# A two-block transformer kernel: one more weight unit split ahead of the wait for x, and TensorE's first feed-forward loop pass written out

## The chip, the cores and the metric

The kernel runs on one NeuronCore of one Trainium2 chip. The metric is the device time of one execution in microseconds; three executions gave 1204.47 to 1204.54, median 1204.53. One further execution was recorded by the hardware profiler and took 1204.95.

## The reference, cut to what matters

Two transformer stages run one after the other on 256 tokens of width 1024, all in fp32. The change touches only the four feed-forward layers, of which the first opens the kernel.

```python
def swiglu(x, w_gate, w_up, w_down):
    return (jax.nn.silu(x @ w_gate) * (x @ w_up)) @ w_down

# first block, D_FF = 2816, FFN_RES = 0.5
h = h + FFN_RES * swiglu(rms_norm(h, ffn1_norm[l]), ffn1_w_gate[l], ffn1_w_up[l], ffn1_w_down[l])
h = h + hybrid_mixer(...)
h = h + FFN_RES * swiglu(rms_norm(h, ffn2_norm[l]), ...)
# second block, two layers, each: mixer, cross-attention, then
x = x + swiglu_2(rms_norm_2(x, g_ffn[layer]), w_gate[layer], w_up[layer], w_down[layer])
```

## The kernel before, in words

Weights come in **units**: 128 partitions by 1024 fp32 values (512 KB), numbered from 0 in the order in which TensorE uses them (TOTAL of them, table STREAM). Each unit passes four hands. SyncE (SP) loads it into a raw slot, in a feed-forward one of six (`loaded[slot]` rises by 32 when both halves are in). ScalarE (ACT) rounds it to the high part `wh` (L741, `high_done`). VectorE (DVE) subtracts to get the low part `wl` (L1360, `low_done`). TensorE then runs 12 matmuls of 512 columns on it (L2035 to L2037: high by high, high by low, low by high) and raises `units_used`. `wh` and `wl` have six slots (NSPLIT), so unit u may be split once unit u - 6 is used. In the code `split(v)` of ScalarE adds LEAD = 4 to v, so `split(u + 2)` with u = 0 is unit 6, the seventh; VectorE's order is the same.

A feed-forward layer has 11 chunks (NFC) of 256 hidden columns. A chunk takes 4 gate/up units and 2 down units. After the gate/up units of a chunk, ScalarE does the SiLU (`silu_step`, L845, two instructions, scaled by `rstd`), VectorE multiplies by the up half (`mul_step`, L1423, which writes `sb_scores` and raises `h_ready` twice a chunk), ScalarE makes two uint16 planes (`planes_step`), a DMA transposes them, VectorE joins them (L1434), ScalarE makes the high part `hTh` and VectorE the low part `hTl` (L1440, `ht_low`). TensorE then uses them on the down units.

TensorE's order in a layer is: gate/up of chunk 0, of chunk 1 (bank 0), then `body(0)` (gate/up of chunk 2 in bank 6, down of chunk 0), then a loop whose pass c does the gate/up of chunk c + 2 in bank 0 and the down units of chunk c. Each loop pass starts with a wait for `h_ready`, so that the bank it overwrites has been read. In the loop that wait is for the value 2·NFC·f + 4 + 2c, in pass 1 the value 6: chunk 2 multiplied. Bank 0, which pass 1 overwrites, holds chunk 1. `start` and `stop` of the accumulation groups, all slots and all other waits are set by constants or by the loop register.

In layer 0 (f = 0) the beginning is special. Units 0 to 5 come from a packed tensor `h_first`, then SP loads x (two halves, `x_in` 16 each), then units 6 and 7 and on. ScalarE splits units 0 to 5, and then needs x for the sum of squares of each token (`token_ssq`, L784, two instructions). GpSimd (POOL) turns the sums into `rstd` (L619, L620), on which `silu_step(0)` waits. All queues are in order: SP's, ScalarE's, VectorE's and TensorE's instructions run in the order in which they stand.

Of the kernel before, what the change touches and what calls it, by code (L numbers as in the profile page):

```python
# [36 lines left out]
NFC = FF // FC  # L37
# [105 lines left out]
def two_block_kernel(nc, d, out):  # L143
    ctx = ExitStack()
    with ctx:
# [3 lines left out]
        def sem(name):  # L149
            return ctx.enter_context(nc.semaphore(name))  # L150
# [157 lines left out]
        h_ready = sem("h_ready")  # L308
# [422 lines left out]
        def _(act):  # L731
# [8 lines left out]
            def copy(dst, src, scale=1.0):  # L740
                return act.activation(dst, src, ACT.Copy, scale=scale)  # L741

            def split(u, c=0):

                u = u + LEAD
                if isinstance(c, int):
                    u, c = u + 6 * c, 0
                    if u >= TOTAL:
                        return

                act.wait_ge(loaded[SLOT[u]], 32 * NTH[u] + 32 * c)
                if u >= NSPLIT:

                    act.wait_ge(units_used, u - NSPLIT + 1 + 6 * c)
                copy(wh[:, u % NSPLIT, :], raws[SLOT[u]]).then_inc(high_done, 1)

            def splits(u, n):
                for i in range(n):
                    split(u + i)
# [27 lines left out]
            def rs(stat, t):  # L787
                return rstd[:, 2 * stat + t:2 * stat + t + 1]
# [51 lines left out]
            def ffn(f, tail=None):  # L840
                u, norm = FIRST[f"ffn{f}"], FFN_NORM[f]

                def silu_step(c, first_bank=0):
                    for t in range(NT):
                        act.activation(silu[:, t, :], bank[first_bank + t][:, 0:FC], ACT.Silu, scale=rs(norm, t))\  # L845
                           .then_inc(silu_done, 1)

                def planes_step(c):

                    act.wait_ge(h_ready, 2 * NFC * f + 2 + 2 * c)  # L850
                    for h in range(2):
                        ins = copy(planes.rearrange("p (h t c) -> p h t c", h=2, t=NT)[:, h], hid_halves[:, h])
                    ins.then_inc(planes_done, 1)

                def turned_step(c, dst):

                    act.wait_ge(hT_joined, NFC * f + c + 1)
                    copy(dst, hT).then_inc(ht_high, 1)

                def turn_hidden():  # L860
                    act.dma_start_transpose(planesT.rearrange("p (b r) -> p b r", r=P), planes).then_inc(planes_turned, 16)

                def hidden(c, v, c6=0):

                    split(v, c6)
                    planes_step(c)

                    act.wait_ge(planes_done, NFC * f + c + 1)
                    split(v + 1, c6)
                    turn_hidden()  # L870

                def body(c, last=False):
                    v = u + 8
                    split(v, c)
                    split(v + 1, c)
                    turned_step(c, hTh[:, :, :])
                    split(v + 2, c)
                    split(v + 3, c)
                    if last:
                        turned_step(c + 1, yTh[:, 6:8, :])  # L880

                    act.wait_ge(units_used, v + 4 + 6 * c)
                    silu_step(c + 2)
                    hidden(c + 2, v + 4, c)

                if f > 0:
                    xt_high(norm, 0)
                    if f > 1:

                        splits(u - 2, 2)  # L890
                    xt_high(norm, 1)
                split(u)
                if f > 0:
                    token_ssq(norm, x)
                    load_tables(SILU_SET)
                split(u + 1)
                if f == 0:

                    act.wait_ge(x_in, 32)
                    token_ssq(norm, x)  # L900
                    split(u + 2)
                rstd_known(norm)

                act.wait_ge(units_used, u + 4 if f > 0 else u + 5)
                silu_step(0, FFN_FIRST_BANK[f])
                n = 2 if f > 0 else 3
                hidden(0, u + n)
                if f == 2:
                    km_split(1, 4)
                    split(u + 4)  # L910
                    km_turn(1)
                for i in range(4 if f in (1, 3) else 5, 8):
                    split(u + i)

                act.wait_ge(units_used, u + 8)
                silu_step(1)
                turned_step(0, hTh[:, :, :])
                hidden(1, u + 8)
                splits(u + 10, 2)

                act.wait_ge(units_used, u + 12)
                silu_step(2, 6)
                hidden(2, u + 12)
                with act.Fori(1, NFC - 3, 1) as c:
                    body(c)
                body(NFC - 3, True)
                split(u + 62)
                turned_step(NFC - 1, aTh[:, 6:8, :])
                split(u + 63)
                if tail is not None:  # L930
                    tail()
                splits(u + 64, 2)
# [1096 lines left out]
        def _(pe):  # L2029
# [85 lines left out]
            def ffn(f, norm_after):  # L2115
                u, norm = FIRST[f"ffn{f}"], FFN_NORM[f]
                acc = [[bank[2 + 2 * n + t] for n in range(2)] for t in range(NT)]

                def down(u_slot, k, n, t, start, stop, high, low):
                    w = slice(512 * n, 512 * n + 512)  # L2120
                    return products(acc[t][n][:, :], high[:, k, tok(t)], low[:, k, tok(t)],
                                    wh[:, u_slot % NSPLIT, w], wl[:, u_slot % NSPLIT, w], start, stop)

                def gate_up(v, bank_, c=0, begun=0):

                    for i in range(begun, 4):
                        square(v + i, 2 * i, aTh, aTl, bank_, i == 0, i == 3, c)

                def down_unit(v, k, high, low, c=0, start=False):

                    pe.wait_ge(low_done, v + 1 + 6 * c)
                    for n in range(2):
                        for t in range(NT):
                            ins = down(v, k, n, t, start, False, high, low)
                    ins.then_inc(units_used, 1)

                def body(c, bank_=0, start=False):
                    if bank_ == 0:

                        pe.wait_ge(h_ready, 2 * NFC * f + 4 + 2 * c)  # L2140
                    gate_up(u + 8, bank_, c)

                    pe.wait_ge(ht_low, NFC * f + 1 + c)
                    for k in range(2):
                        down_unit(u + 12 + k, k, hTh, hTl, c, start and k == 0)

                if f == 0:
                    for i in range(EARLY):
                        early_unit(i, (FFN_FIRST_BANK[f], 0)[FRONT[i][0]], 2 * FRONT[i][1])
                    chunk(u + 1, FFN_FIRST_BANK[f], a_ready(norm), begun=2)  # L2150
                    gate_up(u + 4, 0, begun=1)

                    pe.wait_ge(ident_in, 16)
                else:
                    chunk(u, FFN_FIRST_BANK[f], a_ready(norm), before={1: lambda: xt_half(norm, 1)})
                    gate_up(u + 4, 0)
                body(0, 6, True)
                with pe.Fori(1, NFC - 3, 1) as c:
                    body(c)
                body(NFC - 3)  # L2160

                pe.wait_ge(ht_low, NFC * f + NFC - 1)
                for k in range(2):
                    down_unit(u + 62 + k, k, yTh[:, 6:8, :], yTl[:, 6:8, :])

                pe.wait_ge(ht_low, NFC * f + NFC)

                pe.wait_ge(low_done, u + 66)
                for n in range(2):
                    for t in range(NT):  # L2170
                        if n == 1 and t == 1 and norm_after is not None:
                            xt_half(norm_after, 0)
                        for k in range(2):
                            ins = down(u + 64 + k, k, n, t, False, k == 1, aTh[:, 6:8, :], aTl[:, 6:8, :])
                            if n == 1 and t == 1:
                                ins.then_inc(units_used, 1)
                        if n == 0 or t == 0:
                            ins.then_inc(acc_done, 1)
# [495 lines left out]
```

## Time and profile before

| | before |
|---|---|
| median of 3 executions | 1204.53 us |
| profiled execution | 1204.95 us |
| its span, first to last instruction | 1203.0 us |
| TensorE busy | 1195.1 us, 99% |
| VectorE busy | 780.0 us, 65% |
| ScalarE busy | 699.0 us, 58% |
| GpSimd busy | 73.8 us, 6% |
| DMA, mean | 195 GB/s |

The span is what the profiler's instructions cover; the profiled execution lasted 1.95 us longer. Busy time of TensorE contains the modelled end of each matmul (0.39 us shown for one, while the next starts 0.227 us after it), so where a start comes late, the step between two starts tells more than the idle time that the profile reports.

### The profile page before, as it was taken

How to read it: one execution, taken by the hardware profiler on the slowest of the kernel's cores; microseconds unless marked ns; L12 is line 12 of the kernel's file. 1: busy time of each engine (PE TensorE's matmuls, PEld its weight loads, DVE VectorE, ACT ScalarE, POOL GpSimd, SP SyncE). 2: the span in 40 equal slices, each digit the busy share in tenths (PEclk: the TensorE clock that was granted, in tenths of full speed). 3: DMA queues.
4: the chain of work that ended last, by engine and by line, in shares of the span. 5: the costliest groups of instructions: out<-in, count | busy, mean ns of one | idle time of the engine just before them, and what ended most of it. 6: DMA issues, size and time to landing. Idle time of an engine off the chain costs nothing.

```text
span 1203.0 us, 16864 instructions
## 1 busy us (share of the span) xinstructions
PE 1195.1 (99%) x5622; PEld 986.0 (82%) x5622; DVE 780.0 (65%) x1107; ACT 699.0 (58%) x1030; POOL 73.8 (6%) x119
## 2 busy tenths in 40 slices
PE   9999999999999999999999999999999999999998
PEld 7888888877788888888888788888888887888887
DVE  6656556688686656557778766756556667665554
ACT  7545555566555545558675576645555546755552
POOL 0430000000000000000220110000000000000000
PEclk9999999999999999999999999999999999999999
DMA  9987764554556987755754528977655454876662
GB/s 314 268 235 228 224 200 153 162 168 139 164 193 190 275 248 231 220 179 174 200 171 162 175 60 230 262 226 210 205 175 175 144 163 132 245 225 200 202 200 76
DMA packets 218917, 234.68 MB, mean 195 GB/s; under 512 B 66608, under 2 KB 158896, under 8 KB 218864
## 3 DMA queue, kind: packets, MB, share of 16 engines
q1 hardware_dynamic: 163792, 214.61, 56.9%
q10 hardware_dynamic: 53280, 13.64, 6.3%
q0 software_dynamic: 1792, 5.75, 1.7%
q8 instruction: 31, 0.51, 0.2%
q14 instruction: 22, 0.18, 0.0%
HBM read 219.78 MB, written 1.05 MB: 184 GB/s over the span
## 4 chain that ended last, share of the span: by engine, by line
PE 96%; DMA 2%; DVE 1%; ACT 1%; issue 0%; ACTq 0%; DVEq 0%
PE bank L2035 30%; PE bank L2037 30%; PE bank L2036 30%; PE bank L2094 2%; DMA sb_probs<-sb_probs 1%; PE bank L2248 1%; PE bank L2264 1%; PE bank L2235 1%; PE bank L2233 0%; DMA sb_gates<-h_xT 0%; ACT sb_probs L1277 0%; PE bank L2552 0%; DVE sb_rmax L1930 0%; PE bank L2541 0%; PE bank L2266 0%
## 5 line engine op out<-in xcount | busy, mean ns | idle before, releaser
L1360 DVE TENSOR_TENSOR sb_wl<-sb_raw,sb_wh 128x1024 fp32r<-128x1024 f32 x313 | 376.3, 1222 | 116.5 <-ACT sb_wh L741 111.6
L2035 PE MATMUL bank<-sb_wh,sb_aTh 128*128 128x512 f32 (+1 forms) x1124 | 435.5, 387 | 0.6 <-DVE sb_scores L1423 0.5
L2037 PE MATMUL bank<-sb_wh,sb_aTl 128*128 128x512 f32 (+1 forms) x1124 | 431.0, 383 | 0.0
L2036 PE MATMUL bank<-sb_wl,sb_aTh 128*128 128x512 f32 (+1 forms) x1124 | 430.7, 383 | 0.0
L741 ACT ACTIVATE sb_wh<-sb_raw 128x1024 fp32r<-128x1024 f32 (+1 forms) x319 | 326.9, 1047 | 142.2 <-PE bank L2037 103.0
L2035 PEld LDWEIGHTS bank<-sb_wh,sb_aTh 128*128 128x128 f32 x1124 | 211.3, 188 | 42.2 <-issue 1.4
L2037 PEld LDWEIGHTS bank<-sb_wh,sb_aTl 128*128 128x128 f32 x1124 | 211.2, 188 | 41.9
L2036 PEld LDWEIGHTS bank<-sb_wl,sb_aTh 128*128 128x128 f32 x1124 | 211.4, 188 | 40.1
L1360 DVE TENSOR_TENSOR sb_wl<-sb_z,sb_wh 128x1024 fp32r<-128x1024 f32 x88 | 107.5, 1226 | 56.0 <-ACT sb_wh L741 56.0
L845 ACT ACTIVATE sb_junk<-bank,sb_rstd 128x256 f32<-128x256 f32 x88 | 36.8, 470 | 156.6 <-PE bank L2037 156.3
L1423 DVE SCALAR_TENSOR_TENSOR sb_scores<-bank,sb_rstd,sb_junk 128x256 f32<-128x256 f32 x88 | 38.5, 479 | 115.6 <-ACT sb_junk L845 115.4
L2035 PE MATMUL bank<-sb_wh,sb_hTh 128*128 128x512 f32 x288 | 112.0, 389 | 0.0
L2036 PE MATMUL bank<-sb_wl,sb_hTh 128*128 128x512 f32 x288 | 112.0, 389 | 0.0
L2037 PE MATMUL bank<-sb_wh,sb_hTl 128*128 128x512 f32 x288 | 112.0, 389 | 0.0
L741 ACT ACTIVATE sb_wh<-sb_z 128x1024 fp32r<-128x1024 f32 x88 | 92.8, 1059 | 1.7 <-DMA sb_z<-h_first 0.5
L2035 PE MATMUL bank<-sb_wh,sb_yTh 128*128 128x512 f32 x224 | 89.8, 401 | 0.0
L2037 PE MATMUL bank<-sb_wh,sb_yTl 128*128 128x512 f32 x224 | 87.5, 390 | 0.0
L2036 PE MATMUL bank<-sb_wl,sb_yTh 128*128 128x512 f32 x224 | 87.3, 390 | 0.0
L2036 PEld LDWEIGHTS bank<-sb_wl,sb_hTh 128*128 128x128 f32 x288 | 54.1, 188 | 11.3
L2035 PEld LDWEIGHTS bank<-sb_wh,sb_hTh 128*128 128x128 f32 x288 | 54.0, 188 | 11.2
L2037 PEld LDWEIGHTS bank<-sb_wh,sb_hTl 128*128 128x128 f32 x288 | 54.1, 188 | 11.2
L741 ACT ACTIVATE sb_probs<-sb_scores 128x512 uint16<-128x512 uint16 x88 | 50.4, 625 | 3.3 <-DVE sb_scores L1423 3.2
(220 smaller groups left out, 929.1 us busy)
## 6 DMA issues: line engine op xcount, KB each, us to landing
sb_raw<-ffn_w_down SPq DMA_DIRECT2D x80, 256.0 KB, 4.4
sb_raw<-w_in SPq DMA_DIRECT2D x80, 256.0 KB, 3.2
sb_raw<-w_down SPq DMA_DIRECT2D x80, 256.0 KB, 3.9
sb_raw<-w_gate SPq DMA_DIRECT2D x48, 256.0 KB, 3.2
sb_raw<-w_up SPq DMA_DIRECT2D x48, 256.0 KB, 4.0
sb_raw<-ffn_w_gate SPq DMA_DIRECT2D x44, 256.0 KB, 3.6
sb_raw<-ffn_w_up SPq DMA_DIRECT2D x44, 256.0 KB, 4.4
sb_raw<-e_w_in SPq DMA_DIRECT2D x40, 256.0 KB, 3.3
```

Of the source, the lines that this page charges most:

```text
L741: return act.activation(dst, src, ACT.Copy, scale=scale)
L845: act.activation(silu[:, t, :], bank[first_bank + t][:, 0:FC], ACT.Silu, scale=rs(norm, t))\
L1360: dve.tensor_tensor(wl[:, u % NSPLIT, :], raws[SLOT[u]], wh[:, u % NSPLIT, :].bitcast(F32), ALU.subtract).then_inc(low_done, 1)
L1423: dve.scalar_tensor_tensor(hid[:, t, :], bank[first_bank + t][:, FC:2 * FC], rs(norm, t), silu[:, t, :], ALU.mult, ALU.mult).then_inc(h_re ...
L2035: pe.matmul(dst, lh, w_hi, start=start, stop=False)
L2036: pe.matmul(dst, lh, w_lo, start=False, stop=False)
L2037: return pe.matmul(dst, ll, w_hi, start=False, stop=stop)
L2094: ins = pe.transpose(dst[:, T * j + P * t:T * j + P * t + P], tiles(j, t), ident[:])
L2235: pe.matmul(bank[4 + i % 2][:, P:3 * P], q[:, P:T], k[:, 0:T], start=True, stop=True).then_inc(at.s_psum, 1)
L2248: ins = pe.transpose(bank[6][:, tok(j)], probs[:, i % 4, tok(j)], ident[:])
L2264: pe.matmul(bank[7][r, a:a + T], v[:, 0, c], pT[:, 0:T], start=True, stop=False)
```

## The change

On ScalarE, in layer 0, the split of unit 6 now stands before the wait for x and the two sums of squares instead of behind them. On TensorE, in all four layers, pass 1 of the loop is written out as straight code, and its wait is for `h_ready` at 2·NFC·f + 4 (chunk 1 multiplied), a constant; the loop runs from pass 2.

```diff
                 split(u + 1)
                 if f == 0:
+                    split(u + 2)
 
                     act.wait_ge(x_in, 32)
                     token_ssq(norm, x)
-                    split(u + 2)
                 rstd_known(norm)
...
                 def body(c, bank_=0, start=False):
-                    if bank_ == 0:
+                    if isinstance(c, int) and c == 1:
+
+                        pe.wait_ge(h_ready, 2 * NFC * f + 4)
+                    elif bank_ == 0:
 
                         pe.wait_ge(h_ready, 2 * NFC * f + 4 + 2 * c)
                     gate_up(u + 8, bank_, c)
...
                 body(0, 6, True)
-                with pe.Fori(1, NFC - 3, 1) as c:
+                body(1)
+                with pe.Fori(2, NFC - 3, 1) as c:
                     body(c)
                 body(NFC - 3)
```

ScalarE at the front of layer 0, as a difference of the two orders (the first two rows are units 4 and 5, the L741 row that moves is unit 6, L784 the sums of squares, L845 the SiLU of chunk 0):

```order
 L741 ACTIVATE sb_wh<-sb_z 128x1024 [waits loaded4]
 L741 ACTIVATE sb_wh<-sb_z 128x1024 [waits loaded5]
+L741 ACTIVATE sb_wh<-sb_raw 128x1024 [waits units_used,loaded0]
 L784 ACTIVATE sb_junk,sb_ssq<-sb_x 128x1024 [waits x_in]
 L784 ACTIVATE sb_junk,sb_ssq<-sb_x 128x1024 [waits ssq_done]
-L741 ACTIVATE sb_wh<-sb_raw 128x1024 [waits units_used,loaded0]
 L845 ACTIVATE sb_junk<-bank,sb_rstd 128x256 [waits units_used,rstd_ready]
 L845 ACTIVATE sb_junk<-bank,sb_rstd 128x256
```

Only this one instruction moved, with its waits for the load of unit 6 and for a used slot. The orders of VectorE and SP are the same in both kernels.

TensorE in layer 0 where `body(0)` ends and pass 1 begins, before:

```order
 L2035 MATMUL bank5<-sb_wh,sb_hTh 128x512
 L2036 MATMUL bank5<-sb_wl,sb_hTh 128x512
 L2037 MATMUL bank5<-sb_wh,sb_hTl 128x512
 L2158 UNCONDITIONAL_BRANCH
 L2158 ISA
 L2042 ISA [waits h_ready]
 L2035 MATMUL bank0<-sb_wh,sb_aTh 128x512 [waits low_done]
```

The same place after:

```order
 L2035 MATMUL bank5<-sb_wh,sb_hTh 128x512
 L2036 MATMUL bank5<-sb_wl,sb_hTh 128x512
 L2037 MATMUL bank5<-sb_wh,sb_hTl 128x512
 L2035 MATMUL bank0<-sb_wh,sb_aTh 128x512 [waits low_done,h_ready]
 L2036 MATMUL bank0<-sb_wl,sb_aTh 128x512
 L2037 MATMUL bank0<-sb_wh,sb_aTl 128x512
```

The loop's entry now stands one pass (72 matmuls) later; the matmuls executed are the same in number and order.

## Rows read from the trace of the kernel before

**Rows 1.** The page: the span, busy times, the granted TensorE clock in 40 slices.
```profile
span 1203.0 us, 16864 instructions
PE 1195.1 (99%) x5622; PEld 986.0 (82%) x5622; DVE 780.0 (65%) x1107; ACT 699.0 (58%) x1030; POOL 73.8 (6%) x119
PEclk9999999999999999999999999999999999999999
```

**Rows 2.** Waits of TensorE, whole span: waited for: us in total, times, longest.
```profile
PE bank L2541 <- DVE sb_probs L1944: 2.1, 4, 0.8
PE bank L2035 <- DVE sb_scores L1423: 0.5, 1, 0.5
```

**Rows 3.** Timeline of TensorE, layer 0: start us, us, instruction [idle before].
```profile
1.31 3.78 PE L2192 MATMUL bank<-sb_hTh 128*128 128x512 f32 x8 [1.31 <-POOL sb_half_neg L609]
...
22.30 0.39 PE L2037 MATMUL bank<-sb_wh,sb_aTl 128*128 128x512 f32 x1
22.77 0.50 PE L2035 MATMUL bank<-sb_wh,sb_aTh 128*128 128x512 f32 x1
23.11 0.40 PE L2036 MATMUL bank<-sb_wl,sb_aTh 128*128 128x512 f32 x1
...
28.39 0.39 PE L2035 MATMUL bank<-sb_wh,sb_aTh 128*128 128x512 f32 x1
...
39.27 0.39 PE L2035 MATMUL bank<-sb_wh,sb_hTh 128*128 128x512 f32 x1
...
44.48 0.39 PE L2037 MATMUL bank<-sb_wh,sb_hTl 128*128 128x512 f32 x1
45.34 0.49 PE L2035 MATMUL bank<-sb_wh,sb_aTh 128*128 128x512 f32 x1 [0.47 <-DVE sb_scores L1423]
```

**Rows 4.** Timeline of VectorE, layer 0: units 6, 7, 8, then 34 to 38 us.
```profile
21.49 1.23 DVE L1360 TENSOR_TENSOR sb_wl<-sb_raw,sb_wh 128x1024 fp32r<-128x1024 f32 x1 [3.98 <-ACT sb_wh L741]
...
23.51 1.23 DVE L1360 TENSOR_TENSOR sb_wl<-sb_raw,sb_wh 128x1024 fp32r<-128x1024 f32 x1
25.82 1.23 DVE L1360 TENSOR_TENSOR sb_wl<-sb_raw,sb_wh 128x1024 fp32r<-128x1024 f32 x1 [1.08 <-ACT sb_wh L741]
...
34.20 0.81 DVE L1434 COPY sb_probsT<-sb_probs 128x512 uint16<-128x512 uint16 x2 [3.46 <-DMA sb_probs<-sb_probs]
34.88 0.87 DVE L1423 SCALAR_TENSOR_TENSOR sb_scores<-bank,sb_rstd,sb_junk 128x256 f32<-128x256 f32 x2
...
36.65 1.23 DVE L1360 TENSOR_TENSOR sb_wl<-sb_raw,sb_wh 128x1024 fp32r<-128x1024 f32 x1 [0.25 <-ACT sb_wh L741]
```

**Rows 5.** Busy time in 1060 to 1190 us: length, PE, PEld, DVE, ACT, POOL, PEclk, DMA, GB/s.
```profile
1060.00:1190.00 130.00, 130.00 (x575) 107.67 (x574) 75.18 (x90) 66.40 (x86) 0.00 (x0) 1.00 0.63 190
```

**Rows 6.** TensorE's loop line: duration ns min/median/max, first and last start.
```profile
L2158 PEldq COMPARE_BRANCH  x28: 76/208/236, 57.9 to 1168.4; - x28
```

**Rows 7.** Timeline of ScalarE, layer 0, 18 to 25 us.
```profile
18.17 1.06 ACT L784 ACTIVATE sb_junk<-sb_x 128x1024 f32<-128x1024 f32 x1 [1.92 <-DMA sb_x<-x]
...
20.41 1.04 ACT L741 ACTIVATE sb_wh<-sb_raw 128x1024 fp32r<-128x1024 f32 x1
21.69 0.84 ACT L845 ACTIVATE sb_junk<-bank,sb_rstd 128x256 f32<-128x256 f32 x2 [0.23 <-POOL sb_rstd L620]
22.42 1.06 ACT L741 ACTIVATE sb_wh<-sb_raw 128x1024 fp32r<-128x1024 f32 x1
23.54 1.15 ACT L741 ACTIVATE sb_probs<-sb_scores 128x512 uint16<-128x512 uint16 x2
24.72 1.06 ACT L741 ACTIVATE sb_wh<-sb_raw 128x1024 fp32r<-128x1024 f32 x1
```

**Rows 8.** Timeline of SP's queue: the issue of unit 6's second half.
```profile
11.43 0.47 SPq L488 DMA_DIRECT2D sb_raw<-ffn_w_up  x1
```

**Rows 9.** DMA issues from 11.42 to 11.90 us: KB each, us to landing.
```profile
sb_raw<-ffn_w_up SPq DMA_DIRECT2D x1, 256.0 KB, 8.2
```

**Rows 10.** The chain that ended last, from 24 us: the first transpose.
```profile
24.73 9.44 DMA sb_probs<-sb_probs
```

## The prediction

> **What bounds the kernel now.** I read the page first: TensorE is busy 1195.1 of 1203.0 us, at the full clock in every slice [rows 1]. So a change pays only where it removes a late start of a matmul, and costs only where it makes one. Next I read who TensorE waits for. In the feed-forward layers there is a single entry, 0.5 us on VectorE's multiply; the larger ones are in the cross-attention [rows 2], which the change doesn't touch. Then the timeline of layer 0, by the steps between starts. Undisturbed, 48 matmuls run from 28.39 to 39.27, which is 0.2267 each and 2.72 per unit of 12. Two steps are longer. At unit 6 the step is 22.77 - 22.30 = 0.47, late by 0.24, and the matmul behind it comes after 0.34 instead of 0.227, another 0.11. At pass 1 the step is 45.34 - 44.48 = 0.86, late by 0.63 [rows 3]; I add 0.11 for the restart there too, after unit 6's. Together 0.35 + 0.74 = 1.09 us is all that the two edits can give back.
>
> **The wait at pass 1 (second edit).** In layer 0 pass 1 waits for chunk 2 multiplied; it now waits for chunk 1, multiplied at 34.88 + 0.87 = 35.75 [rows 4], over 9 us before TensorE gets there. The other wait there, for unit 14, was no bar: no further idle time follows it. So the edit takes 0.74 off as long as chunk 1 is in time. In layers 1 to 3 no such step exists, and from 1060 to 1190 us, nearly the whole loop of layer 3 and what follows it, TensorE is busy 130.00 of 130.00 [rows 5]. There is nothing to take there: 0.
>
> **The pass written out.** It removes one taken branch and a few register instructions per layer, 4 in all, and adds no executed matmul. Branches take 0.21 us median, 0.24 at most [rows 6], yet there are seven per layer (28 in all), and the stretch of layer 3 shows no idle time [rows 5]: they are decoded while matmuls already queued run. I take 0. From below the bound is 4 x 0.24 = 0.96 us gained, if each had been exposed; from above I take the same 0.96 us as a loss, one such stall per layer for fetching the longer code. The value is 0, for the straight code of `body(0)` runs at 0.2267 per matmul as the loop does [rows 3, 5]. The Trainium skill (Runtime: NRT & Kernel Launch, Instruction fetch mechanics) says that a taken branch to a target outside the fetched window stalls the engine, which is why kernels prefer unrolling. By that rule four stalls go and the sum below would come out near zero instead; the trace disagrees, with 130.00 busy of 130.00 in looped code [rows 5].
>
> **The split of unit 6 ahead of x (first edit).** This step decides the sign. ScalarE is in order. Before, it waits for x until 18.17, does both sums of squares, and starts unit 6 at 20.41 [rows 7]. For the split to be free in front of x, unit 6 would have to be in by about 17. But SP issues it behind x: its second half goes out at 11.43 and lands 8.2 us later [rows 8, 9], at 19.6 to 19.7. Nothing that decides this landing is changed. So ScalarE now sits until 19.66, splits until about 20.65 (a following instruction starts about 0.98 after one of 1.06), and only then starts the sums of squares, which wait for nothing any more. They start 20.65 - 18.17 = 2.48 us late. The split itself ends 0.73 earlier.
>
> What follows, each row moved by 2.48:
> - The sums end 20.41 -> 22.89 and the SiLU of chunk 0 goes from 21.69 to 24.17. Before, the split of unit 6 ran in the 1.28 us in which GpSimd made `rstd`; that cover is now empty time.
> - Unit 7's split stands behind the SiLU: 22.42 -> 24.90 [rows 7]. Its low part starts 23.51 -> 25.99 and ends at 27.22 [rows 4].
> - Unit 6 itself: high part at about 20.65, low part at 21.95, wanted at 22.53. The late start of 0.35 is gone.
> - TensorE wants unit 7 at 22.53 + 2.72 = 25.25 and gets it at 27.22 + 0.05 = 27.27 (unit 6 began 0.05 behind its low part: 21.49 + 1.23 = 22.72, 22.77). Stall 2.02, restart 0.11: +2.13.
> - Unit 8 begins at 27.27 + 2.72 + 0.11 = 30.10, before 28.39. Its low part was ready at 25.82 + 1.23 = 27.05, now 29.53: 0.57 in hand.
> - Chunk 0's transpose. It took 9.44 from 24.73 [rows 10]; issued at 27.21 with the same 9.44 it lands at 36.65 instead of 34.17, and chunk 1 is multiplied by 38.2. `hTl` of chunk 0 and unit 12 (36.65 + 1.23 = 37.88 before [rows 4], 40.36 then) are wanted at 40.98, the 39.27 of before plus 1.71. 0.6 us in hand, and none of these has a price.
>
> At pass 1: 30.10 + 48 x 0.2267 + 24 x 0.2267 = 46.42. Before, pass 1 started at 45.34 and had 0.11 of restart. Here the second edit acts: chunk 1 is ready at 38.2, so there is no wait, while chunk 2 (a transpose later) would have come at about 45.2 + 2.5 = 47.7 and cost 1.3 with the old wait.
>
> **The sum.** First edit: -0.35 + 2.13 = +1.78. Second: -0.74. Writing out: 0. Net +1.04, or by starts 46.42 - 45.34 - 0.11 = +0.97; the two differ by rounding, and I take +1.0. Later waits are relative to TensorE and move along with it. The profiled execution took 1204.95, so its like would be 1205.95. The median runs are 0.42 shorter: 1204.53 + 1.0 = **1205.5 us**. A change of under 0.2%, 2.4 us, can't be told from none for this kernel; this is such a one, with a sign of slower.
>
> **Rivals.**
> *Both edits give what they can.* If unit 6 were in when ScalarE asks, or if the delayed sums were absorbed, the time would be 1204.53 - 1.09 = 1203.4. For it: unit 6's own wait does vanish, and the second edit is sound by itself. Against: an 8.2 us landing behind x, and only 25.67 - 24.74 = 0.93 us of lead of unit 7 over TensorE against 2.48 of delay [rows 3, 4, 9]. Chance 0.14.
>
> *Branches were exposed.* Then 0.96 us comes off the +1.0 and the time is 1204.57. For it only that a branch takes 0.2 us; against it the stretch without idle time. The skill's rule on branches, cited above, is this case. Chance 0.04.
>
> *More of the chain is late.* The 0.57 and 0.6 us in hand at units 8 and 12 are used up, for instance by a first transpose that takes 1 us longer still, as it would then run beside the loads of units 13 to 15. That adds 0.4 to 1.2: 1205.9 to 1206.7, say 1206.3. For it: the transpose did take 9.44 us under load. Against: it now starts when the load backlog of the front is over, so it should be shorter. Chance 0.12.
>
> *Slower beyond doubt: the clock falls.* A stall of 2.0 us at 25 us, where the longest of before within the kernel is 0.8 [rows 2] and the clock stayed at its high level of 2.4 GHz [rows 1]. If the granted clock falls to 1.2 GHz there, matmuls start 0.43 apart, as the first eight did (3.78 us for 8 with the last one's end [rows 3]), instead of 0.227. It took some 4 us of such matmuls to rise again after the start, so 9 or 10 matmuls lose 0.2 each: +1.9, and with +1.0 the sum is +2.9, or 1207.4. It decides once an idle stretch longer than any of before is enough to lower the clock. Against: all 40 slices at full clock despite waits, and 2 us is little more than twice what was borne. Chance 0.06. The Trainium skill (TensorE: Matmul & The Clock Gate, HAM oscillation — how this bites in real kernels) says that waits for data between bursts of matmuls let the clock drop to half; the trace has no idle stretch of 2 us, so it bears out neither side.
>
> **How the numbers follow.** My forecast 0.64, full gain 0.14, late chain 0.12, clock 0.06, exposed branches 0.04. The range runs from the full gain, 1203.4, to the upper part of the late chain, 1206.6; outside it lie the clock case and what is left of extra stalls. The unknown cost of the written-out pass, 0.96 either way, keeps the forecast within 1204.5 to 1206.5, inside the range. Faster by over 0.2% would need more than the two late starts hold: 0.01. Slower by over 0.2% is the clock case and the far tail of the late chain: 0.06. Within 0.2%: 0.93.
>
> **What would show it.** In the new timeline: ScalarE idle on the load of unit 6 until about 19.7; the sums of squares at about 20.7; the SiLU at 24.2; TensorE stopping at 25.25 for about 2.0 us on VectorE's low part of unit 7 (start 27.3); no late start at unit 6 and none at pass 1, which begins near 46.4; full clock throughout; from there on every landmark 1.0 later than before. Sums of squares still at 18.2 would make me wrong and the kernel 1.1 us faster; a start of pass 1 later than 47 would show the late chain; starts 0.43 apart behind 27 us the clock.

## The result and the profile after

The changed kernel took 1206.49 us, median of 22 runs (1205.10 to 1208.11), against 1204.49 for the kernel before in 22 runs (1203.49 to 1205.14): +2.0 us, ratio 1.0016 with a 95% interval of 1.0010 to 1.0022, or +1.2 to +2.7 us. The prediction was 1205.5 in a range of 1203.4 to 1206.6. The sign and the stall are as forecast, the size is twice it.

The page of the changed kernel, with the span and busy times (answers to [rows 1]):

```profile
span 1204.9 us, 16832 instructions
PE 1194.8 (99%) x5622; PEld 985.8 (82%) x5622; DVE 779.7 (65%) x1107; ACT 698.8 (58%) x1030; POOL 72.9 (6%) x119
```

TensorE does the same work in 1.9 us more of span. The waits of TensorE (us in total, times, longest; to [rows 2]) name two things in layer 0 that were not there:

```profile
PE bank L2545 <- DVE sb_probs L1944: 2.1, 4, 0.8
PE bank L2063 <- ACT sb_wh L741: 1.5, 1, 1.5
...
PE bank L2035 <- DVE sb_wl L1360: 1.3, 1, 1.3
```

The 1.3 us on `sb_wl` is the forecast stall. The 1.5 us on L2063 lies in the first 9 us, before anything that the change touches. The kernel before has that wait too, shorter in its profile, in a row that the prediction passed over when it read TensorE's waits:

```profile
PE bank L2063 <- ACT sb_wh L741: 0.6, 1, 0.6
```

The timelines of ScalarE and TensorE after (start us, us, instruction; to [rows 7] and [rows 3]):

```profile
20.34 1.06 ACT L741 ACTIVATE sb_wh<-sb_raw 128x1024 fp32r<-128x1024 f32 x1 [3.43 <-DMA sb_raw<-ffn_w_up]
21.31 1.04 ACT L784 ACTIVATE sb_junk<-sb_x 128x1024 f32<-128x1024 f32 x1
...
24.81 0.84 ACT L845 ACTIVATE sb_junk<-bank,sb_rstd 128x256 f32<-128x256 f32 x2 [1.19 <-POOL sb_rstd L620]
25.54 1.06 ACT L741 ACTIVATE sb_wh<-sb_raw 128x1024 fp32r<-128x1024 f32 x1
```

```profile
15.56 0.39 PE L2035 MATMUL bank<-sb_wh,sb_aTh 128*128 128x512 f32 x1
...
26.21 0.39 PE L2037 MATMUL bank<-sb_wh,sb_aTl 128*128 128x512 f32 x1
27.91 0.50 PE L2035 MATMUL bank<-sb_wh,sb_aTh 128*128 128x512 f32 x1 [1.31 <-DVE sb_wl L1360]
28.25 0.39 PE L2036 MATMUL bank<-sb_wl,sb_aTh 128*128 128x512 f32 x1
...
47.10 0.39 PE L2035 MATMUL bank<-sb_wh,sb_aTh 128*128 128x512 f32 x1
```

ScalarE sits 3.43 us on the load of unit 6, the sums of squares follow, and where GpSimd makes `rstd` ScalarE is now idle for 1.19 us instead of 0.23. TensorE stops ahead of unit 7 for 27.91 - 26.21 - 0.23 = 1.47 us, plus 0.11 at the restart. There is no late start at unit 6 nor at pass 1 (47.10). But unit 3 starts at 15.56, not 14.27: the whole front of this execution is 1.3 us later. This is not the change's doing: the second profile of the changed kernel, at the end, has unit 3 at 14.32. So the front varies from one execution to the next, which made me doubt the profile of before as the basis.

### The profile page after: what moved, and what is told of

Read it like the earlier page. It is cut to its first block, busy times and chain, and to the rows that moved or that the text cites. A ratio compares the mean times of both kernels' runs of the same rounds, so it can differ in the third digit from the quotient of the medians.

```text
span 1204.9 us, 16832 instructions
## 1 busy us (share of the span) xinstructions
PE 1194.8 (99%) x5622; PEld 985.8 (82%) x5622; DVE 779.7 (65%) x1107; ACT 698.8 (58%) x1030; POOL 72.9 (6%) x119
## 3 DMA queue, kind: packets, MB, share of 16 engines
q0 software_dynamic: 1792, 5.75, 1.6%
## 4 chain that ended last, share of the span: by engine, by line
PE 96%; SPq 1%; ACT 1%; DVE 1%; DMA 1%; issue 0%; POOL 0%; POOLq 0%
PE bank L2035 30%; PE bank L2037 30%; PE bank L2036 30%; PE bank L2094 2%; PE bank L2252 1%; DMA sb_raw<-ffn_w_up 1%; PE bank L2268 1%; PE bank L2239 1%; SPq L546 1%; PE bank L2237 0%; ACT sb_probs L1277 0%; PE bank L2556 0%; DVE sb_rmax L1930 0%; PE bank L2545 0%; PE bank L2270 0%
## 5 line engine op out<-in xcount | busy, mean ns | idle before, releaser
L741 ACT ACTIVATE sb_wh<-sb_raw 128x1024 fp32r<-128x1024 f32 (+1 forms) x319 | 326.6, 1047 | 145.7 <-PE bank L2037 105.5
L845 ACT ACTIVATE sb_junk<-bank,sb_rstd 128x256 f32<-128x256 f32 x88 | 37.0, 471 | 158.3 <-PE bank L2037 157.1
L741 ACT ACTIVATE sb_wh<-sb_z 128x1024 fp32r<-128x1024 f32 x88 | 92.8, 1059 | 1.7 <-DMA sb_z<-h_first 0.5
L741 ACT ACTIVATE sb_probs<-sb_scores 128x512 uint16<-128x512 uint16 x88 | 50.4, 626 | 2.1 <-DVE sb_scores L1423 2.1
```

## The experiments

"u3" below is the start of unit 3 on TensorE, the first matmul behind the three early units; "u6" is the landing of unit 6. From u3 to pass 1 there are 132 matmuls, 29.92 us undisturbed. Each time is a median of 11 runs (9 for the last), beside runs of the kernel before on the same chip. An interval of the ratio of 0.0009 either way is 1.1 us either way, so a difference of a few tenths can be read only from the traces.

One sum helps to read all of them. In 12 of the 14 profiles the profiled time less the start of pass 1 lies between 1159.4 and 1159.7 us, from 1204.95 - 45.34 for the first profile to 1206.82 - 47.10 for the changed kernel. So whatever these kernels gain or lose, they gain or lose before pass 1 of layer 0. The two exceptions are the two kernels under "An early front".

**Each edit alone.** First edit alone: only ScalarE's part of the diff.

```diff
                 if f == 0:
+                    split(u + 2)
 
                     act.wait_ge(x_in, 32)
                     token_ssq(norm, x)
-                    split(u + 2)
```

> First edit alone: unit 6 split ahead of the wait for x, loop and its wait as before. Theory (the delayed sums of squares stall TensorE on unit 7): unit 6's high part starts when its load lands, about 20 us, TensorE stops before unit 7 by 1.5 to 2.0 us and reaches pass 1 so late that chunk 2 is multiplied by then, so the old wait costs little; time as with both edits, 1206.0 to 1206.5 against 1204.5. Rival (the written-out pass carries part of the loss): 0.5 to 1.0 us less than with both edits, 1205.5 or below.

Measured: 1206.09 against 1204.52, ratio 1.0012 (1.0003 to 1.0021). The first edit alone carries the loss of about 1.6 us. Its trace has the same stop:

```profile
27.15 0.50 PE L2035 MATMUL bank<-sb_wh,sb_aTh 128*128 128x512 f32 x1 [1.26 <-DVE sb_wl L1360]
```

It starts 1.42 us late, and pass 1, with the old wait for chunk 2, starts without a gap at 46.34. The old wait costs nothing here: in this trace chunk 2 is multiplied by 44.23, over 2 us before TensorE arrives. The prediction had put it at 47.7, and 1.3 us of wait with it; but the two transposes, issued later, took 6.0 and 6.1 us to land and not 9.4 and 5.9.

Second edit alone: only TensorE's part of the diff.

```diff
-                    if bank_ == 0:
+                    if isinstance(c, int) and c == 1:
+                        pe.wait_ge(h_ready, 2 * NFC * f + 4)
+                    elif bank_ == 0:
...
-                with pe.Fori(1, NFC - 3, 1) as c:
+                body(1)
+                with pe.Fori(2, NFC - 3, 1) as c:
```

> Second edit alone: pass 1 written out with the wait for chunk 1, the split of unit 6 where it was. Theory: the late start at pass 1 (0.74 us with its restart) is gone, nothing else moves: 1203.8 against 1204.5. Rival (written-out code costs about 1 us somewhere): 1204.8 or more.

Measured: 1204.68 against 1204.52, ratio 1.0000 (0.9991 to 1.0009). My 0.7 us of gain did not show, though the interval of 1.1 us either way would still hold it. The trace says why there was nothing to gain in this execution: chunk 2 was multiplied by 43.29 and pass 1 began at 45.55, so the old wait would have been over as well. The time is near the rival's 1204.8, but the next kernel shows that its reason is not the one.

**Written out, old wait.**

```diff
-                with pe.Fori(1, NFC - 3, 1) as c:
+                body(1)
+                with pe.Fori(2, NFC - 3, 1) as c:
```

> Pass 1 written out, but with the old wait for chunk 2; split of unit 6 where it was. Theory: writing out is free, and the late start at pass 1 of about 0.6 us stays: 1204.5, no change. Rival (written-out code costs): 1205.0 to 1205.5.

Measured: 1204.58 against 1204.52, ratio 0.9999 (0.9990 to 1.0008). Straight code costs nothing that can be measured, nor do its four branches fewer bring anything. But its trace refutes the other half of my expectation: with the old wait there is no late start either. VectorE multiplies chunk 2 here (second row below) by 43.57, and pass 1 starts at 45.06, 29.92 behind u3 at 15.14:

```profile
42.02 0.81 DVE L1434 COPY sb_probsT<-sb_probs 128x512 uint16<-128x512 uint16 x2 [0.67 <-DMA sb_probs<-sb_probs]
42.70 0.87 DVE L1423 SCALAR_TENSOR_TENSOR sb_scores<-bank,sb_rstd,sb_junk 128x256 f32<-128x256 f32 x2
```

**Unit 6 loaded ahead of x.** Both edits, and on SP's queue:

```diff
+                load_gate_up(6, 0, FRONT[6][1], FRONT[6][0])
                 for t in range(NT):
                     sp.dma_start(x[:, t, :], xv[:, t, :]).then_inc(x_in, 16)
-                for u in range(6, 8):
-                    load_gate_up(u, 0, FRONT[u][1], FRONT[u][0])
+                load_gate_up(7, 0, FRONT[7][1], FRONT[7][0])
```

> Both edits, and SP loads unit 6 ahead of x instead of behind it. Theory: unit 6 lands near 17, its split ends before x is in; x now lands where unit 6 did, near 19.7 to 20, so the sums of squares are 1.5 us later than in the kernel before, not 2.5; the stall at unit 7 shrinks to about 1.0 us, and the time is 1.0 us below both edits alone: 1205.0 to 1205.5, or 1204.6 by the rows of the kernel before (-0.35 -0.74 +1.14). Rival (the loss is not in the sums of squares): no gain against both edits, 1206.5.

Measured: 1205.17 against 1204.52, ratio 1.0004 (0.9995 to 1.0013). ScalarE's timeline shows the trade:

```profile
17.64 1.06 ACT L741 ACTIVATE sb_wh<-sb_raw 128x1024 fp32r<-128x1024 f32 x1 [0.86 <-DMA sb_raw<-ffn_w_up]
20.21 1.06 ACT L784 ACTIVATE sb_junk<-sb_x 128x1024 f32<-128x1024 f32 x1 [1.51 <-DMA sb_x<-x]
```

Unit 6 is now split while x is still on its way, and x decides. The sums start 20.21 - 14.76 = 5.45 us behind u3, against 21.31 - 15.56 = 5.75 in the changed kernel, and TensorE's stop at unit 7 is 1.10 us instead of 1.47. The time is 0.9 below the first edit alone on the same chip.

**The kernel before, once more.** No edit.

> The kernel before once more, for a second profile. Theory now (the two late starts of the first profile came from a front that was early that time, with unit 3 at 14.27 us where later profiles have 14.8 to 15.6): unit 3 starts at 14.8 to 15.6, no late start or a much smaller one at unit 6 and at pass 1, and the time is 1204.5. Rival (the late starts are a fixed property of this kernel, and the second edit failed for another reason): steps of about 0.47 and 0.86 at unit 6 and pass 1 again, wherever unit 3 starts.

Measured: 1204.23 against 1204.45, ratio 1.0000. TensorE around unit 6 and at pass 1:

```profile
22.20 0.39 PE L2035 MATMUL bank<-sb_wh,sb_aTh 128*128 128x512 f32 x1
22.43 0.39 PE L2036 MATMUL bank<-sb_wl,sb_aTh 128*128 128x512 f32 x1
22.66 0.39 PE L2037 MATMUL bank<-sb_wh,sb_aTl 128*128 128x512 f32 x1
22.88 0.39 PE L2035 MATMUL bank<-sb_wh,sb_aTh 128*128 128x512 f32 x1
...
44.42 0.39 PE L2037 MATMUL bank<-sb_wh,sb_hTl 128*128 128x512 f32 x1
44.64 0.39 PE L2035 MATMUL bank<-sb_wh,sb_aTh 128*128 128x512 f32 x1
```

Every step is 0.22 or 0.23. u3 is 14.72, and from there to pass 1 it is 29.92. The two late starts of the first profile [rows 3] are not in this execution of the same kernel. They have different reasons.

At unit 6 the front decides. In the first profile u3 was 14.27, so TensorE wanted unit 6 at 22.53, and its low part was ready at 22.72. Here it wanted it at 22.88, and the low part was ready at 21.19 + 1.23 = 22.42.

At pass 1 the front doesn't decide: without the wait TensorE would have begun it at 44.71 in the first profile, and here it did at 44.64. What differs is chunk 2. Here are the issues of the two transposes that it stands behind and its own multiply, in the first profile and then in this one:

```profile
24.73 1.31 ACTq L861 DMA_TRANSPOSE sb_probs<-sb_probs  x1
37.70 1.25 ACTq L861 DMA_TRANSPOSE sb_probs<-sb_probs  x1
44.34 0.86 DVE L1423 SCALAR_TENSOR_TENSOR sb_scores<-bank,sb_rstd,sb_junk 128x256 f32<-128x256 f32 x2
```

```profile
24.43 1.32 ACTq L861 DMA_TRANSPOSE sb_probs<-sb_probs  x1
36.67 1.25 ACTq L861 DMA_TRANSPOSE sb_probs<-sb_probs  x1
42.48 0.86 DVE L1423 SCALAR_TENSOR_TENSOR sb_scores<-bank,sb_rstd,sb_junk 128x256 f32<-128x256 f32 x2
```

The transposes took 9.4 and 5.9 us from issue to landing in the first profile and 8.7 and 5.0 here, so chunk 2 was multiplied at 45.20 there and at 43.34 here. That late start was time lost: the first profiled execution took 1204.95, this one 1204.20, and its pass 1 began 0.70 later. The prediction was read from an execution 0.5 us above the median of its kernel.

**Unit 7 split early too.** Both edits, and on ScalarE and VectorE (an excerpt; the counts of the splits behind are adapted to it):

```diff
                     token_ssq(norm, x)
+                    split(u + 3)
                 rstd_known(norm)
...
                 if f == 0:
-                    split(u + 2)
+                    splits(u + 2, 2)
                 mul_step(0, FFN_FIRST_BANK[f])
```

> Both edits, and the split of unit 7 moved too, on ScalarE between the sums of squares and the wait for rstd, on VectorE ahead of the multiply of chunk 0. Theory (the loss is unit 7's split behind a late SiLU and nothing else): no stall at unit 7, the time falls by 1.6 to 2.0 to that of the kernel before, 1204.3 to 1204.7. Rival (the delayed chain costs elsewhere, at unit 8 or chunk 0's transpose): the wait turns up there and over 1205.3 remains.

Measured: 1204.13 against 1204.45, ratio 0.9999 (0.9990 to 1.0008): 0.3 below its neighbours of the kernel before, which is inside the noise, where the changed kernel is 2.0 above them. All of the loss is gone: pass 1 starts 29.92 behind u3, as in the second profile of the kernel before. ScalarE still waits 3.44 us for unit 6, but unit 7 no longer stands behind the SiLU:

```profile
19.84 1.06 ACT L741 ACTIVATE sb_wh<-sb_raw 128x1024 fp32r<-128x1024 f32 x1 [3.44 <-DMA sb_raw<-ffn_w_up]
...
23.03 1.04 ACT L741 ACTIVATE sb_wh<-sb_raw 128x1024 fp32r<-128x1024 f32 x1
24.31 0.84 ACT L845 ACTIVATE sb_junk<-bank,sb_rstd 128x256 f32<-128x256 f32 x2 [0.24 <-POOL sb_rstd L620]
```

The SiLU itself is as late as in the changed kernel (24.31 here; 24.05 to 24.81 in the three profiles with the first edit and the old loads), so its lateness is harmless; the loss was unit 7's alone.

**An early front.** The kernel before, and one load moved from ScalarE's queue to SP's, behind unit 1:

```diff
-            act.dma_start(xT[:, 2:4, :], xt_piece(2, 4)).then_inc(xt_in[2], 16)
...
                 for u in range(EARLY):
                     load_early_unit(u)
+                    if u == 1:
+                        load_xt(2, 2, 4)
```

> The kernel before, with one load moved: the 256 KB piece of x transposed (tiles 2 and 3) goes out on SP's queue behind unit 1 instead of on ScalarE's beside unit 0, to make the front earlier. Theory: unit 0's second half and tile 1 land up to 0.7 us earlier, unit 3 starts near 14.4, but the late starts at unit 6 and pass 1 come back and take 0.3 to 0.7 of it: 1204.2 to 1204.5. Rival (the front is not bound by these loads): nothing moves, unit 3 at about 15.1.

> Both edits, unit 7's split moved as in the last but one, and the front's load moved as in the last. Theory: with an early front the two late starts would come back, and here nothing is left of them, so the gain of the front is kept whole: unit 3 near 14.4, pass 1 29.92 us later at 44.3, 1203.7 to 1204.0, 0.4 to 0.8 below the kernel before. Rival: the same as the front alone.

The second of these is the kernel with unit 7 split early, plus the same move. Measured: 1204.95 (ratio 1.0004, 0.9995 to 1.0013) and 1204.67 (1.0005, 0.9996 to 1.0014), against 1204.45. The front did come early, u3 at 13.93 and 13.85. With the old order both late starts are back, at unit 6 a step of 0.48 and at pass 1 one of 0.37; with unit 7 split early, pass 1 starts at 44.02. At pass 1 it is again chunk 2 that is late, multiplied at 44.31 behind a first transpose of 9.9 us. But no time is won, against my 1203.7 to 1204.0 for the second kernel, since new stalls stand far behind. In the second kernel:

```profile
575.22 0.39 PE L2039 MATMUL bank<-sb_wh,sb_aTl 128*128 128x512 f32 x1
575.94 0.50 PE L2037 MATMUL bank<-sb_wh,sb_aTh 128*128 128x512 f32 x1 [0.34 <-DVE sb_aTl L1780]
...
754.17 0.50 PE L2037 MATMUL bank<-sb_wh,sb_aTh 128*128 128x512 f32 x1 [0.76 <-DVE sb_wl L1362]
```

The other kernel has the first of these stalls too (a step of 0.91 at 576) and not the second. On ScalarE's queue the issue of a transpose, 14 us earlier, takes longer in both. In the second kernel:

```profile
562.01 2.88 ACTq L811 DMA_TRANSPOSE sb_probsT<-sb_probs  x1
```

and in the kernel before, second profile:

```profile
562.62 1.33 ACTq L809 DMA_TRANSPOSE sb_probsT<-sb_probs  x1
```

**The same early front, each queue with its old number of DMAs.** The load stays on ScalarE's queue, but behind its first split:

```diff
-            act.dma_start(xT[:, 2:4, :], xt_piece(2, 4)).then_inc(xt_in[2], 16)
...
             early_split(0, 0)
+            act.dma_start(xT[:, 2:4, :], xt_piece(2, 4)).then_inc(xt_in[2], 16)
```

> Both edits, unit 7's split moved, and the 256 KB piece of x transposed issued on ScalarE's own queue as before, only later, behind its first split, so that each queue keeps its number of DMAs. Theory: the front is early (unit 3 at 13.9 to 14.4), pass 1 is at 43.8 to 44.3, and the issue of the transpose at 562 us takes under 1.5 us again as in all kernels with that number of DMAs on the queue, so no stall at 576 us: 1203.4 to 1203.9. Rival (the stalls at 576 and 754 us come with an early front itself): a step over 0.5 us at 576 again, 1204.5 or more.

> Second edit alone (pass 1 written out, waits for chunk 1), with the same early front as the last kernel. Theory: with an early front the second edit now pays: a late start remains at unit 6 (0.2 to 0.4) and none at pass 1, 0.1 to 0.5 below the kernel before with the same front. Rival: equal to it.

> The kernel before with the same early front alone. Theory: late starts at unit 6 (about 0.25) and pass 1 (0.1 to 0.6) return as in the first profile, 0.3 to 0.9 above both edits with unit 7 moved and this front: 1204.2 to 1204.5. Rival: no late starts, the same time as those.

The three bases are both edits with unit 7 split early, the second edit alone, and the kernel before. Measured, against 1204.57 for the kernel before: 1204.11 (ratio 0.9993, 0.9984 to 1.0002), 1204.04 (0.9996, 0.9987 to 1.0005) and 1204.22 (0.9997, 0.9988 to 1.0006). The issue at 562 us takes 1.33 us again and the stall at 576 is gone in all three, so the stall goes with the long issue and not with the early front. How the one leads to the other was not followed step by step. The front was less early than hoped, u3 14.20, 14.68, 14.56, and the first time missed its forecast of 1203.4 to 1203.9. So the differences that I had forecast between the three, 0.3 to 0.9 us, shrank to 0.2, which can't be told from none. In the first of them, with u3 at 14.20, TensorE then stopped at unit 12 instead (step 0.52), behind a first transpose of 8.3 us. None of the versions beats the kernel before by more than its interval.

**The changed kernel, once more.** No further edit.

> Both edits, the changed kernel once more, for a second profile and more runs. Theory: the stall at unit 7 is set by the time from the start of unit 3 to the landing of unit 6, less 3.29 us (after: 20.32 - 15.56 = 4.76 and 1.47 us of stall; first edit alone: 19.56 - 14.84 = 4.72 and 1.42 us), within 0.15 us; no late start at unit 6 or pass 1; pass 1 begins 26.8 us after unit 6's landing; time 1206.0 to 1206.5, and 1.5 to 2.0 above the kernel before. Rival (something besides adds to it, since both edits ran 0.4 above the first alone): a further step in the trace, and 1206.5 or more.

Measured: 1206.78 in 9 runs against 1204.31 in 13, ratio 1.0021 (1.0011 to 1.0031). The time is above the 1206.0 to 1206.5 that I expected. The formula for the stall held: u6 - u3 = 19.73 - 14.32 = 5.41, less 3.29 is 2.12; the stop is 27.32 - 25.07 - 0.23 = 2.02. And the rival held too, by a further loss that the prediction had priced. TensorE behind the stop:

```profile
25.07 0.39 PE L2037 MATMUL bank<-sb_wh,sb_aTl 128*128 128x512 f32 x1
27.32 0.50 PE L2035 MATMUL bank<-sb_wh,sb_aTh 128*128 128x512 f32 x1 [1.86 <-DVE sb_wl L1360]
...
28.95 0.63 PE L2035 MATMUL bank<-sb_wh,sb_aTh 128*128 128x512 f32 x1
29.38 0.63 PE L2036 MATMUL bank<-sb_wl,sb_aTh 128*128 128x512 f32 x1
29.80 0.63 PE L2037 MATMUL bank<-sb_wh,sb_aTl 128*128 128x512 f32 x1
...
32.24 0.39 PE L2037 MATMUL bank<-sb_wh,sb_aTl 128*128 128x512 f32 x1
32.47 0.39 PE L2035 MATMUL bank<-sb_wh,sb_aTh 128*128 128x512 f32 x1
```

Starts 0.43 apart: from about 28.9 to 32.0 the granted clock was at its low level of 1.2 GHz, 0.51 over the window below. The windows of this run (length, busy times by engine, then PEclk, DMA share and GB/s) before, in and after it:

```profile
14.00:27.00 13.00, 11.26 (x49) 8.93 (x48) 6.47 (x9) 8.04 (x12) 0.90 (x2) 1.00 1.09 361
28.60:32.00 3.40, 3.40 (x10) 2.62 (x9) 3.20 (x4) 3.10 (x4) 0.00 (x0) 0.51 1.09 240
32.20:44.00 11.80, 11.80 (x53) 9.77 (x53) 9.21 (x14) 7.21 (x12) 0.86 (x1) 1.00 1.06 308
```

Pass 1 starts at 48.11, which is 14.32 + 29.92 + 2.02 of stall + 0.19 of two slow second matmuls + 1.66 of slow clock. Less those 1.66, pass 1 would have begun at 46.45.

How often this happens is known less well, since only this one execution with it has a profile. The mean granted clock is 0.999 instead of 1.000 in 5 of the 31 runs of the changed kernel, and these are its five slowest, 1207.32 to 1208.67; the other 26 are 1205.10 to 1207.01. In none of the 121 runs of the eleven other experiments was it below 1.000. But it was 0.999 in 3 of the 106 runs of the kernel before beside them as well, and these took 1204.16, 1204.23 and 1204.25, no longer than their neighbours. So the mean alone doesn't mark such an execution. For the four runs without a profile the fallen clock is likely, by their times, and not shown.

## Why the prediction was right in kind and half the size

*The split of unit 6 ahead of x, +1.78.* Right as a mechanism in every link: ScalarE waits for the load behind x, the sums of squares and SiLU move by it, unit 7 comes late, and the last hand-offs have slack. Moving unit 7 alone removed the whole loss. With u3 at 14.3, as in the profile that I read, the stall is the predicted 2.02 to a hundredth, and pass 1, less the clock's part, is at 46.45 where the prediction had 46.42. In the two other profiles with this edit and the old loads u3 was 0.5 to 1.3 us later and the stall 1.42 and 1.47.

*The late starts given back, -0.35 and -0.74.* This is the term that was mis-sized: for the median it should have been close to 0. I took both from one execution and applied them to the median. In the four profiles of kernels with the old split order and the old loads, u3 was 14.27 (both late starts), 14.72, 15.14 and 15.63 (none). The start at unit 6 is late when the front is early. The one at pass 1 is late when chunk 2 is: multiplied at 45.20 in the first profile, and at 43.34, 43.56 and 43.29 in the three others, by the time that the two transposes took. By these times the second edit could have saved its 0.74 in that one execution, and nothing in the others. With this term at 0 the sum is +2.13, and the measured +2.0 lies beside it.

*What the size depends on.* With the first edit and the old loads pass 1 began 26.8 us behind u6 in both profiles at full clock, wherever u3 was. Without the edit it began 29.92 behind u3 where nothing was late. So the cost in one execution is about u6 - u3 - 3.1, which gives 1.6, 1.6 and 2.3 us in the three profiles. How these two times lie in the runs without a profile is not known. So it is open why the changed kernel's median is 2.0 above and that of the first edit alone 1.6, and the two intervals overlap.

*The range.* 1206.49 lies inside it only because its upper part, to 1206.6, was drawn for a late chain of units and transposes, which did not come. That is luck.

*Writing pass 1 out, 0.* Right: +0.06 with the old wait, inside the noise. In the trace of the changed kernel pass 1 as straight code lasts 63.42 - 47.10 = 16.32 us, and pass 2 in the loop 79.74 - 63.42 = 16.32. The Trainium skill (Runtime: NRT & Kernel Launch, Instruction fetch mechanics) speaks of taken branches whose target lies outside the fetched window. The prediction charged the four branches by that rule without a row that shows where their targets lie. What the runs show is only that four branches fewer bring nothing that can be measured.

*The clock.* I gave it 6 in 100 as a rival for the whole result. It is true in one profiled execution, likely in four more of the 31, and the others show no sign of it. It doesn't carry the median: without these five runs the changed kernel's is 1206.47. My price was +1.9, the trace has 1.66. In that trace the clock fell behind a stall of 2.02 us; in the traces with stalls of 1.10, 1.42 and 1.47 it did not, and one case doesn't show that the length decides. The Trainium skill (TensorE: Matmul & The Clock Gate, HAM oscillation — how this bites in real kernels) says that waits for data between bursts of matmuls can drop the clock to half; this one trace agrees, with 0.51 behind a wait of 2.02 us. The prediction took the pace from the slow first eight matmuls of the kernel; the pace was right, but for those eight the trace shows no low clock, for between 2 and 4 us the granted clock reads 1.00.

*The late chain, third rival.* Unit 8 kept 0.8 us in hand, and chunk 0's transpose took about 6 us instead of 9.44 when issued later, as I had argued against it. It showed only at unit 12 with an early front.

## What to carry to other kernels

Before an instruction is moved ahead of a wait on an in-order engine, ask whether its own input has arrived by then, that is where its load stands in the queue relative to the thing waited for. Here the split moved in front of a load that was queued behind x, and it turned 1.3 us of useful cover into 3.4 us of idle time. And a late start that one profile shows is not yet time to be had: take a second profile of the same kernel, and compare when the input of the late instruction is ready. Here one of the two late starts came with an early front, and the other with two transposes that were slow in the one execution and faster in the next.

## What the runs showed of the hardware that was not expected

The first loads of a kernel land at different times in each execution. In the eight profiles of kernels that issue these loads identically, the second half of unit 0 landed between 4.7 and 6.9 us, and unit 3 started between 14.27 and 15.63.

The first transpose of the kernel, with the old split order, took 9.4, 9.5 and 9.9 us to land in the three profiles where unit 3 started at 14.27, 14.56 and 13.93, and 7.5 to 8.7 in the four where it started between 14.68 and 15.63. Whether the early front makes it slow is not shown.

The issue time of a DMA transpose went with what had gone through its queue earlier. The one at 562 us took 1.33 us in twelve profiles with the usual number of DMAs on ScalarE's queue, and 3.04 and 2.88 in the two with one DMA fewer; in both ScalarE's next instruction started when it was over. The one at 746 us varied with no change to the queue, from 3.38 to 4.55. With one DMA fewer it took 3.32 and 5.54, the latter in the kernel that stalled at 754. Why the issue time depends on this is open.
